# Two stationary tensors of a transformer kernel at sixteen start offsets modulo 512 bytes

## The reference

```python
# first block
xn = rmsnorm(h, norm_mix_g); u = xn @ w_in            # 1024 x 7168: q k v xr gr ga gb
ya = chunked_band_attention(q, k, v) @ w_attn_out
yb = (rg_lru(conv(xr)) * gelu(gr)) @ w_rnn_out
h = h + (g_a * ya + g_b * yb) @ w_o
g, up = split(rmsnorm(h, norm_ffn_g) @ w_ffn_in)      # 1024 x 5632
h = h + (silu(g) * up) @ w_ffn_out                    # 2816 x 1024
x = rmsnorm(h, final_norm_g)
# second block
h = x + 0.5 * rms_norm(swiglu(rms_norm(x)))           # FFN 1024 -> 2816 -> 1024
z = rms_norm(h) @ w_in_2                              # 1024 x 1952
h = h + rms_norm(concat(neighbourhood_att(z), latent_att(z)) @ w_out_2)
h = h + 0.5 * rms_norm(swiglu(rms_norm(h)))           # another FFN
```

## Time and profile before

| | us |
|---|---|
| time, median of 2 runs | 944.27 (944.06 to 944.48) |
| span of the profiled execution | 942.5 |
| PE busy (matmuls) | 934.1 |
| PEld busy (loads of stationary tiles) | 786.1 |
| DVE busy | 506.8 |
| ACT busy | 494.6 |
| POOL busy | 282.8 |

### The profile page before, as it was taken

The page is one execution under the profiler, slowest core; times in us unless marked ns, Lnnn a source line. Parts: engine busy times, 40 slices in busy tenths (PEclk is TensorE's granted clock), DMA queues, the critical chain, the costliest instruction groups (busy, mean ns, idle before and its releaser), DMA issues.

```text
span 942.5 us, 14135 instructions
## 1 busy us (share of the span) xinstructions
PE 934.1 (99%) x4854; PEld 786.1 (83%) x4854; DVE 506.8 (54%) x845; ACT 494.6 (52%) x797; POOL 282.8 (30%) x140
## 2 busy tenths in 40 slices
PE   9999999999999999999999999999999999999997
PEld 8999977788888888888888888888889878888886
DVE  6868967755654434523733443456486864333323
ACT  6688456644454444444644444447364664444441
POOL 0000000000144444444244444654450044444442
PEclk9999999999999999999999999999999999999999
DMA  8755575355556666786666665655512356565661
GB/s 256 243 179 179 176 232 185 114 173 185 170 180 185 183 190 212 253 228 188 203 188 188 183 192 187 219 160 159 174 62 90 112 164 191 188 190 182 179 198 69
DMA packets 132788, 169.36 MB, mean 180 GB/s; under 512 B 16731, under 2 KB 88446, under 8 KB 132614
## 3 DMA queue, kind: packets, MB, share of 16 engines
q1 hardware_dynamic: 132582, 168.67, 57.7%
q10 hardware_dynamic: 160, 0.07, 0.0%
HBM read 167.61 MB, written 1.10 MB: 179 GB/s over the span
## 4 chain that ended last, share of the span: by engine, by line
PE 97%; ACT 1%; DVE 1%; issue 1%; DVEq 0%; POOLq 0%; POOL 0%; ACTq 0%
PE acc L872 26%; PE acc L874 26%; PE acc L873 26%; PE tp L948 5%; PE acc L930 3%; PE acc L932 3%; PE acc L934 3%; PE acc L1279 1%; PE acc L1016 1%; PE sc L1234 1%; PE sc L1084 1%; PE tp L1103 1%; PE sc L1224 0%; DVE w_lo L1364 0%; PE sc L966 0%
## 5 line engine op out<-in xcount | busy, mean ns | idle before, releaser
L513 ACT ACTIVATE w_hi<-w_raw 128x1024 fp32r<-128x1024 f32 x300 | 317.2, 1059 | 345.6 <-PE acc L874 311.1
L2007 POOL TENSOR_TENSOR w_lo<-w_raw,w_hi 128x1024 fp32r<-128x1024 f32 x106 | 257.5, 2429 | 547.5 <-ACT w_hi L513 547.4
L1364 DVE TENSOR_TENSOR w_lo<-w_raw,w_hi 128x1024 fp32r<-128x1024 f32 x194 | 246.5, 1275 | 267.9 <-ACT w_hi L513 267.0
L872 PE MATMUL acc<-w_hi,xt_hi 128*128 128x512 f32 x704 | 279.8, 397 | 0.6 <-DVE w_lo L1364 0.3
L874 PE MATMUL acc<-w_lo,xt_hi 128*128 128x512 f32 x704 | 274.5, 390 | 0.0
L873 PE MATMUL acc<-w_hi,xt_lo 128*128 128x512 f32 x704 | 274.1, 389 | 0.0
L872 PEld LDWEIGHTS acc<-w_hi,xt_hi 128*128 128x128 f32 x704 | 132.2, 188 | 30.9 <-issue 4.4
L874 PEld LDWEIGHTS acc<-w_lo,xt_hi 128*128 128x128 f32 x704 | 132.1, 188 | 28.2
L873 PEld LDWEIGHTS acc<-w_hi,xt_lo 128*128 128x128 f32 x704 | 132.4, 188 | 25.6
L872 PE MATMUL acc<-w_hi,hid_hi 128*128 128x512 f32 x264 | 103.3, 391 | 0.0
L874 PE MATMUL acc<-w_lo,hid_hi 128*128 128x512 f32 x264 | 102.8, 389 | 0.0
(11 more groups left out here) (218 smaller groups left out, 953.4 us busy)
## 6 DMA issues: line engine op xcount, KB each, us to landing
w_raw<-in_ffn_w_gu SPq DMA_DIRECT2D x172, 256.0 KB
w_raw<-in_w_in SPq DMA_DIRECT2D x68, 512.0 KB
w_raw<-in_w_ffn_in SPq DMA_DIRECT2D x88, 256.0 KB
w_raw<-in_ffn_w_down SPq DMA_DIRECT2D x44, 512.0 KB
w_raw<-in_w_ffn_out SPq DMA_DIRECT2D x22, 512.0 KB
w_raw<-in_w_rnn_out SPq DMA_DIRECT2D x8, 512.0 KB
w_raw<-in_w_attn_out SPq DMA_DIRECT2D x8, 512.0 KB
w_raw<-in_w_o SPq DMA_DIRECT2D x8, 512.0 KB
```

The lines of the kernel that those rows point to most:

```text
L513: act.activation(w_hi[:, b, :], w_raw[:, b, :], ACT.Copy).then_inc(hi_done[b], 1)
L872: pe.matmul(o, hi[:, k, rows], wh, start=first and n == 0, stop=False)
L1364: dve.tensor_tensor(w_lo[:, b, :], w_raw[:, b, :], w_hi[:, b, :].bitcast(F32), ALU.subtract).then_inc(lo_done[b], 1)
L2007: pool.tensor_tensor(w_lo[:, b, :], w_raw[:, b, :], w_hi[:, b, :].bitcast(F32), ALU.subtract).then_inc(lo_done[b], 1)
```

## The change

The rows of xt_hi and xt_lo become eight elements (32 bytes) longer, without these being used, and xt_lo begins 256 bytes behind a multiple of 512. So tile k of xt_hi begins at 32k modulo 512, tile k of xt_lo at 256 + 32k, k from 0 to 7: sixteen different offsets where there was one. All that is placed behind the two moves by 1,024 bytes (and keeps its offset modulo 512). No instruction is added or taken away.

```diff
-    xt_hi = place("xt_hi", [P, KT, T], F32R)
-    xt_lo = place("xt_lo", [P, KT, T], F32R)
+    xt_hi = place("xt_hi", [P, KT, T + 8], F32R)[:, :, 0:T]
+    top[0] = (top[0] + 511) // 512 * 512 + 256
+    xt_lo = nc.alloc_sbuf_tensor_at("xt_lo", [P, KT, T + 8], F32R, offset=top[0])[:, :, 0:T]
+    top[0] = (top[0] + KT * size_of(T + 8) + 511) // 512 * 512
```

## The result

| | before | after |
|---|---|---|
| time, median of 2 runs, us | 944.27 (944.06 to 944.48) | 951.78 (951.53 to 952.03) |
| span of the profiled execution, us | 942.5 | 949.7 |

The ratio is 1.0077 with a 95% interval of [1.0047, 1.0106]: slower by 7.5 us, and clear of zero.

What follows compares the result with a forecast made beforehand. PE was taken as the bound, through the distance between product starts. +8.0 us (512 columns) and +1.3 us (turned), writes 0, on a 942.5 us span plus 1.8 us gave 953.6 us; range 928 to 966, likeliest case 948 to 960.

Steps and rivals of the forecast that it cites:

- The bound: Whole kernel: PE is 97% of the chain; time is the number of products times the distance between their starts.
- Does an offset matter: Auxiliary slabs (bias2, u2 ahead) stream from 128, x tiles at 0: eleven steps of 231.8 ns, unsettled, against 226.7 settled.
- The rival "nothing": Fixed tile-swap cost; auxiliary slabs' pace comes from the stream's own start at 128; time stays 944.3 us; chance 0.34.
- The modulus: Stationary tile and stream count as unequal when their start offsets differ modulo 512 bytes.
- First term, +8.0 us: Products with x stationary and 512 columns: 1,573 settled steps go from 226.7 to 231.8 ns, 5.1 ns each.
- The other 515: Remaining 512 column products with x stationary, already unsettled, waiting or before a turning; not counted in the +8.0 us.
- Second term, +1.3 us: Turned groups, x streaming 256 columns: 768 steps, each +1.7 ns, the middle of 0 and +3.3.
- the 416 wide group's +3.3 ns: Eleven steps with auxiliary slabs, second half streaming from 1,664 bytes: 190.0 ns each against 186.7.
- The outer bound on the negative side: Turned groups: each of the 768 steps could at most lose its whole excess, -13.3 ns.
- The sum: Whole kernel: +9.3 us on the 942.5 us span, with 1.8 us carried over, gives 953.6 us; unsettled case 0.42.
- Faster by a clash removed: Rival: load and stream at equal offsets clash; spreading them saves 25.0 us on 2,745 products, 919.3 us; chance 0.14.
- Much slower from starts at 32 bytes: Rival: x tiles starting off a multiple of 64 cost +13.3 ns on 1,573 and 768 products, +31 us, 975.4 us; chance 0.10.

Runs made afterwards that it cites:

- e6: Against the kernel before, every tile of xt_hi and xt_lo put at 128 bytes modulo 512, w slabs at 0: 953.49 us, ratio 1.0096.
- e7: Against the kernel before, x tiles and the slabs of w_hi and w_lo all at 32 bytes modulo 512, hid and c tiles at 0: 950.70 us, ratio 1.0065.
- e2: Against the kernel before, every tile of xt_hi and xt_lo at 256 bytes modulo 512, w slabs at 0: 944.42 us, ratio 1.0004.
- e10: Against the kernel before, only the w slabs of the turned groups (x streaming, 256 columns) start at 224 bytes modulo 512, x at 0: 942.51 us, ratio 0.9980.

## Why the prediction was right, and where its steps were off

- **The bound.** That the time is the number of products times the distance of their starts held: the spans' 7.2 us are found in those distances, the waits, the clock and the writes did not move.
- **Does an offset matter.** The reading of the auxiliary slabs was the whole basis, and its conclusion held: unequal offsets keep PE out of the settled regime, 231.8 ns in the earlier trace rows and 232.4 in the changed kernel. The evidence was thinner than I took it for. The eleven steps begin one product behind a wait, and products at equal offsets take up to ten to settle behind an interruption (301.43 to 303.83 us in the kernel before), so only the last two of the eleven speak for an effect at all. That it came out is in part luck; e6, where the same auxiliary slabs settle, is the test that the reading lacked. The rival "nothing", which put the auxiliary slabs' pace down to the stream's own start, is refuted by e7, where a stream at 32 runs settled over tiles at 32.
- **The modulus.** "Differ modulo 512" was wrong; e2 has a difference of 256 at no cost. All the rows showed was 0 and 128, and I took the number from the wording of the change. It did not hurt here since fourteen of the sixteen offsets are unequal modulo 256 too (I had fifteen).
- **First term, +8.0 us.** It measured +9.0. Taken one by one, the 1,573 settled products went from 226.7 to 232.3 rather than 231.8 ns, 5.6 ns each, +8.8 us; the sample of eleven steps was a little too cheap. The other 515, taken as unchanged, gave +0.1.
- **Second term, +1.3 us, failed in sign.** "The middle" between 0 and the 416 wide group's +3.3 ns was taken for a shape with no unequal row. It measured -1.3 us: unequal offsets take the settled 256 wide products from 120.0 ns to 116.7 to 118.7, according to the difference. The outer bound on the negative side was in the sum, the value was not, and the sign given for it, turned groups at 120 to 124 ns, failed (118.7). The +3.3 ns was also misread: behind the 128 of the auxiliary slabs the second half of the 416 wide group begins at 128 + 1,664 = 1,792 bytes, a multiple of 256, so half of those eleven steps were at equal offsets, and they too begin just behind a wait.
- **The sum.** +9.3 forecast, +7.5 measured, 953.6 against 951.8 us. The two misses, +1.0 and -2.6 us, have opposite signs and partly cancel; that the total is only 1.8 us off is luck to that extent.
- **Faster by a clash removed.** A gain appeared with 256 columns alone and took at most some 3 of the 13.3 ns (116.7 in e10's stretch); with 512 columns no offset brought the mean below 226.7. Whether that gain is a clash removed is not shown. The rule of the Trainium skill that PE's two read ports are independent ("TensorE: Matmul & The Clock Gate", section "Step-by-step: what each phase is for") would have had no offset matter; 953.2 against 944.4 us for 32 against 256 bytes says that load and stream do affect each other here.
- **Much slower from starts at 32 bytes.** Refuted: 32, 64 and 128 cost the same, 9.0 to 9.2 us.

Not settled: why the settled regime has 13.3 ns too much whatever the columns, and why unequal offsets cost with 512 columns and gain with 256. I name no structure of the memory, since no run isolates one. Alone, differences other than 0, 32, 64, 128, 224 and 256 were not tried, nor starts off a multiple of 32, nor other types than fp32r.

## What to carry to other kernels

Where PE is the bound and its products go at an even pace, and they are 512 columns wide, place stationary and streamed operands at the same offset modulo 256 bytes; here a difference cost 2.8% of each 512 wide product (226.7 to 233 ns), one operand in three was enough, and padding the rows of one operand alone does just that. This is one kernel on one core, with fp32r operands and a load before every product, so measure it in yours. For 256 wide products a difference gained 1 to 3 ns, and e10, with it in the turned stage alone, is the fastest version (942.51 us). And read the pace from starts, over ten or more products and away from the last interruption: the mean durations (391 ns with hid, 393 to 401 with x) hide it.

## What the runs showed that I had not expected

- The difference (stream less stationary tile) counts modulo 256 bytes and, with 256 columns, with its sign: settled turned products 116.7 ns for +32 by two placements, 118.3 ns for -32 by two; 117.8 for 64 and 118.7 for 128 (means over starts later than 68 us).
- The same inequality slows 512 wide products by 6 to 7 ns and speeds up 256 wide ones by 1 to 3 ns, also within one stage and with the same tiles (c in e7).
- The loss is nearly whole with a third of the loads unequal (8.4 of 9.0 us).
